# A two-layer encoder with expert-choice experts in fp32: nine row blocks in the second weight home, its first load in five pieces, a shorter router, later scaling of the norm weights, and the last head one expert later

## The reference

```python
def expert_choice_ffn(h, router_w, wg, wu, wd):
    C = max(1, EC_CAPACITY_FACTOR * S // N_EXPERTS)          # 2*256/16 = 32
    aff = jax.nn.softmax((h @ router_w).astype(jnp.float32), axis=-1)
    gate, idx = lax.top_k(jnp.swapaxes(aff, 1, 2), C)
    xs = take tokens idx of h                                # (16, 32, 1024)
    a = jnp.einsum('becd,edf->becf', xs, wg)                 # 1024 -> 1408
    u = jnp.einsum('becd,edf->becf', xs, wu)
    o = jnp.einsum('becf,efd->becd', jax.nn.silu(a) * u, wd) * gate
    return scatter-add of o to the tokens idx
...
for l in range(DEPTH):
    xn = rms_norm(x, norm1_w[l]); cols = xn @ w_in[l]
    attn = mla_branch(...)        # q and k are RMS-normed with q_norm_w, k_norm_w
    hy = hyena_branch(...)
    merged = gates[:, :, 0] * (attn @ w_attn_branch[l]) + gates[:, :, 1] * (hy @ w_hyena_branch[l])
    x = x + merged @ w_out[l]
    x = x + expert_choice_ffn(rms_norm(x, norm2_w[l]), router_w[l], ...)
```

## Time and profile before

| | |
|---|---|
| median of 3 runs | 2019.53 us (2016.12 to 2020.48) |
| the profiled execution | 2022.94 us, of it the span 2019.3 us |
| PE busy | 1560.6 us (77%) |
| DVE / ACT / POOL busy | 563.2 / 289.1 / 45.7 us |
| queue q1 (SP's transfers) | 638.40 MB, 75.0% of 16 DMA engines |
| mean TensorE clock granted | 0.891 of full |

### The profile page before, as it was taken

One profiled execution on the slowest core, in us unless ns is written; L12 is line 12 of the kernel. 1 busy time (PEld: TensorE's weight loads), 2 busy tenths in 40 slices (PEclk: granted clock), 3 DMA queues, 4 the chain that ended last, 5 costly groups with the idle time before them and its releaser, 6 DMA issues.

```text
span 2019.3 us, 22260 instructions
## 1 busy us (share of the span) xinstructions
PE 1560.6 (77%) x9564; PEld 869.8 (43%) x9564; DVE 563.2 (28%) x1079; ACT 289.1 (14%) x602; POOL 45.7 (2%) x24
## 2 busy tenths in 40 slices
PE   7999999776656665675799999997766666666667
PEld 5687688432222232232256876884222222222222
DVE  2654782211211111111136547612111112111111
ACT  2243210100000000000032332101100000000000
POOL 0300100000000000000002000000000000000000
PEclk9999999897887887798899999998878878878879
DMA  8532054689999999999965221535999999999997
GB/s 290 192 121 84 1 215 181 242 353 433 431 436 430 434 431 430 431 438 433 410 227 229 84 84 49 232 156 209 427 438 424 435 436 435 423 434 437 435 432 316
DMA packets 24378, 644.04 MB, mean 319 GB/s; under 512 B 2672, under 2 KB 3696, under 8 KB 5104
## 3 DMA queue, kind: packets, MB, share of 16 engines
q1 hardware_dynamic: 23248, 638.40, 75.0%
q10 hardware_dynamic: 1056, 4.53, 0.8%
HBM read 641.88 MB, written 1.05 MB: 318 GB/s over the span
## 4 chain that ended last, share of the span: by engine, by line
DMA 49%; PE 47%; DVE 2%; issue 1%; DVEq 1%; ACT 0%; SPq 0%; ACTq 0%
DMA region<-w_down_dram 47%; PE ps L831 11%; PE ps L462 7%; PE ps L529 6%; PE ps L669 5%; PE ps L742 3%; PE ps L490 2%; DMA qkw<-qkw_dram 2%; PE ps L652 1%; PE ps L605 1%; PE ps L552 1%; PE ps L507 1%; PE ps L641 1%; PE ps L790 1%; PE ps L576 1%; PE ps L544 1%
## 5 line engine op out<-in xcount | busy, mean ns | idle before, releaser
L790 PE MATMUL ps<-ring,uT 128*32 128x384 f32 (+1 forms) x3328 | 337.4, 541 | 261.5 <-DMA ring<-w_gbu_dram 254.1
L790 PEld LDWEIGHTS ps<-ring,uT 128*32 128x32 f32 x3328 | 139.9, 125 | 454.0 <-DMA ring<-w_gbu_dram 272.9
L831 PE MATMUL ps<-region,uT 128*32 128x512 f32 x1408 | 225.0, 760 | 94.7 <-DMA region<-w_down_dram 92.1
L1416 DVE TENSOR_TENSOR uT<-uT,ps 128x256 f32<-128x256 f32 x32 | 13.5, 421 | 625.8 <-PE ps L790 625.8
L462 PE MATMUL ps<-xnT,ring 128*128 128x256 f32 x768 | 178.3, 380 | 4.3 <-DVE uT L1074 2.6
L831 PEld LDWEIGHTS ps<-region,uT 128*32 128x32 f32 x1408 | 55.9, 135 | 241.5 <-issue 160.1
L462 PEld LDWEIGHTS ps<-xnT,ring 128*128 128x128 f32 x768 | 140.6, 190 | 23.9 <-DVE uT L1074 4.4
L846 PE MATMUL ps<-uT 128*128 128x512 f32 x256 | 124.1, 617 | 27.6 <-ACT uT L1058 21.6
L1052 ACT ACT_TABLE_LOAD x32 | 41.1, 1283 | 664.9 <-PE ps L790 664.9
L529 PE MATMUL ps<-xnT,ring 128*128 128x256 f32 x512 | 115.8, 380 | 0.0
L1422 DVE COPY uT<-ps 128x512 f32<-128x512 f32 x32 | 22.1, 691 | 303.6 <-PE ps L831 303.6
(11 more groups left out here) (198 smaller groups left out, 1459.8 us busy)
## 6 DMA issues: line engine op xcount, KB each, us to landing
ring<-w_gbu_dram SPq DMA_DIRECT2D x28, 7040.0 KB, 31.0
region<-w_down_dram SPq DMA_DIRECT2D x28, 5632.0 KB, 32.9
ring<-w_ga_dram SPq DMA_DIRECT2D x16, 4224.0 KB, 28.1
region<-w_ga_dram SPq DMA_DIRECT2D x16, 4224.0 KB, 33.4
ring<-units_dram SPq DMA_DIRECT2D x28, 2048.0 KB, 8.1
region<-w_down_dram SPq DMA_DIRECT2D x8, 2048.0 KB, 12.6
region<-units_dram SPq DMA_DIRECT2D x6, 2048.0 KB, 12.3
ring<-w_gbu_dram SPq DMA_DIRECT2D x2, 4992.0 KB, 14.8
```

Of the source, the lines that this page charges most:

```text
L790: m = mm(bank(b, QW[j], rows=CAP, row0=CAP * j), xs[:, i, q * CAP:(q + 1) * CAP], w[i][:, j * FT:j * FT + QW[j]], start=i == 0, stop=i == ...
L831: m = mm(bank(c, rows=CAP, row0=CAP * j), hT[:, b * P + CAP * j:b * P + CAP * (j + 1)], wd[:, CT * b + j, c * 512:(c + 1) * 512], start=b ...
```

## The change

1. **Head of nine row blocks.** `IA` becomes 9: the head now holds all 8 gate row blocks and the first of up (12672 columns), and `w_gbu` only the other 7 of up (9856 columns). The second home in `region` grows over the region's end into what was `uT`, which now lies right behind in the same tensor; the expert scratch (`xs`, `o_sb` and others) is moved 2944 columns on (`SCR`), and a few small tiles to a tensor `late`. `gate_a` is now signalled after the first up row block; a new `gate_h` after gate row block 4.
2. **First load of the second home (head 1) in five pieces**, as its parts come free: 3584 columns after the sixth merged block, 5120 after the eighth, 1024 and 896 behind the down weights of expert 0, and 2048 after the router's first product. **Head 2** comes in two pieces, after `gate_h` and `gate_a` of expert 0.
3. **Last head one expert later**: head 15 is started in the loop's turn 15 ahead of `w_gbu` 15, no longer in turn 14.
4. **Router**: the search reads PSUM directly (no copy); no running sum along tokens on DVE: the marked array is transposed first (PE), compared with 0 (DVE, 128x32), and summed by two matmuls with a triangular and an all-ones matrix. `lgT` is copied ahead of the reciprocal; ACT does its second pair of scaled copies ahead of the second pair of squares. PE runs 4 extra matmuls of 256 columns (`WARM`) whose result nobody reads, once the normalised x is there.
5. **xs in halves**: gate row blocks 0 to 3 wait only for the first half of `xs`.
6. **Norm weights**: the scaling of the q norm weights stands behind the first sine argument.

```diff
-IA = 6
-UP_TAIL = IA - (DB - IA)
+IA = DB + 1
+UP_TAIL = 5
...
-                load_gate_a(0)
+                load_gate_a_first(slice(UNIT, A_COLS))
                 unit_is_used(11)
                 unit_is_used(12)
                 sp.wait_ge(s["merged_dve"], L * 8 + 3)
-                load_gate_b_up_first(0)
+                load_gate_b_up(0)
+                sp.wait_ge(s["merged_dve"], L * 8 + 6)
+                load_gate_a_second(12 * 1024, 12 * 1024 + SPARE)
                 unit_is_used(13)
-                load_gate_b_up_first(1)
+                load_gate_a_first(slice(0, UNIT))
                 for b in range(FB):
                     unit_is_used(RING_UNITS + b)
                     load_down_block(0, b, wd_in[0])
+                    if b == 0:
+                        sp.wait_ge(s["merged_dve"], (L + 1) * 8)
+                        load_gate_a_second(REGION - 3072, REGION + 2048)
+                load_gate_a_second(NF_TILES * D, 12 * 1024)
+                load_gate_a_second(REGION + 2048, REGION + SCR)
                 sp.wait_ge(s["lgT_psum"], L + 1)
-                sp.wait_ge(s["norm2_rms"], L + 1)
-                load_gate_a(1)
+                load_gate_a_second(12 * 1024 + SPARE, REGION - 3072)
                 for e in range(1, E):
-                    if e < E - 1:
+                    if e == 1:
+                        sp.wait_ge(s["gate_h"], L * E + 1)
+                        load_gate_a_third(slice(0, 4 * FF), s["wga_third_in"])
+                        sp.wait_ge(s["gate_a"], L * E + 1)
+                        load_gate_a_third(slice(4 * FF, A_COLS), wga_in[0])
+                    elif e < E - 2:
                         sp.wait_ge(s["gate_a"], L * E + e)
                         load_gate_a(e + 1)
+                    elif e == E - 1:
+                        sp.wait_ge(s["gate_a"], L * E + e - 1)
+                        load_gate_a(e)
...
+                pe.wait_ge(s["xn2_act"], L + 1)
+                for _ in range(WARM):
+                    mm(bank(0, S), ident, xn2[:, 0, 0:S], start=True, stop=True)
+                pe.wait_ge(s["left_dve"], L + 1)
                 for t in range(SB):
-                    m = tp(bank(7, E, t * E), ptok[:, t * P:(t + 1) * P], ident[0:E, 0:E])
-                m.then_inc(s["pos_psum"], 1)
+                    m = tp(bank(7, E, t * E), work[:, t * P:(t + 1) * P], ident[0:E, 0:E])
+                m.then_inc(s["leftT_psum"], 1)
+                pe.wait_ge(s["picked_dve"], L + 1)
+                tri = cst[:, C_TRI:C_TRI + P]
+                mm(bank(6, SB * E, S), tri, picked, start=True, stop=False)
+                mm(bank(6, E, S + E), ones.to_broadcast([P, P]), picked[:, 0:E], start=False,
+                   stop=True).then_inc(s["rank_psum"], 1)
...
-                        for i in range(IA):
+                        for i in range(DB):
+                            if q == 0 and i % 4 == 0:
+                                pe.wait_ge(s["xs_dve"], 2 * (L * NG + g) + i // 4 + 1 + FREE)
                             m = product(2, wg[q % 2], i)
-                        m.then_inc(s["gate_a"], 1)
+                            if i == 3:
+                                m.then_inc(s["gate_h"], 1)
...
-                        for i in range(DB):
+                        product(3, wu[q % 2], 0).then_inc(s["gate_a"], 1)
+                        pe.wait_ge(s["wgbu_in"], 16 * (L * E + 1 + e))
+                        for i in range(1, DB):
...
-                dve.wait_ge(s["qkw_in"], 16 * (L + 1))
-                ts(qkw[:, 0:QK], qkw[:, 0:QK], QK ** -0.5, None, ALU.mult).then_inc(s["qkw_scaled"], 1)
...
                 sine_argument(L, 0)
+                dve.wait_ge(s["qkw_in"], 16 * (L + 1))
+                ts(qkw[:, 0:QK], qkw[:, 0:QK], QK ** -0.5, None, ALU.mult).then_inc(s["qkw_scaled"], 1)
```

More of the change, by code:

```diff
@@ L41 @@
 HW = 512
+WARM = 4
 EPS = 1e-6
@@ L84 @@
 C_FEAT = C_IF + 4 * P
-C_N = C_FEAT + S
+C_TRI = C_FEAT + S
+C_N = C_TRI + P
 NK = NF // 4
@@ L120, in build @@
         xnT_t = sb("xnT", DB * S)
-        uT_t = sb("uT", 24 * S)
+        uT_t = region[:, REGION:REGION + 24 * S]
+        late = sb("late", FT + 80)
         cst = sb("consts", C_N)
@@ L168, in build @@
         mT = uT_t[:, 2048:4096].rearrange("p (i s) -> p i s", s=S)
[L170 to L185 removed]
+        xs = uT_t[:, SCR:SCR + 1024].rearrange("p (i c) -> p i c", i=DB)
+        o_sb = uT_t[:, SCR + 1024:SCR + 2048]
+        gsel = uT_t[:, SCR + 2048:SCR + 2304].rearrange("p (b c) -> p b c", b=SB)
+        gselT = uT_t[:, SCR + 2304:SCR + 2560]
+        sil = uT_t[:, SCR + 2560:SCR + 2560 + FT]
+        hid_e = sil
+        pick = uT_t[:, SCR + 2560 + FT:SCR + 2816 + FT].rearrange("p (b c) -> p b c", b=SB)
+        hT = late[:, 0:FT]
+        lgT = o_sb[:, 0:S]
+        work = o_sb[0:E, S:2 * S]
+        picked = o_sb[:, 2 * S:2 * S + SB * E]
+        top8 = late[0:E, FT:FT + 8]
+        aff = late[:, FT + 16:FT + 16 + SB * E].rearrange("p (b e) -> p b e", b=SB)
+        pos = late[:, FT + 48:FT + 48 + SB * E].rearrange("p (b e) -> p b e", b=SB)
         ones = cst[:, C_ONES:C_ONES + 1]
@@ L205, in build @@
         ksq_rows = aT_t[:, :].rearrange("p (r c) -> p r c", c=NOPE)
-        pos_flat = uT_t[:, 5440:5440 + SB * E]
+        pos_flat = late[:, FT + 48:FT + 48 + SB * E]
         sg = [ring[:, M1AT + i * 512:M1AT + (i + 1) * 512] for i in range(3)]
@@ L1373, in _ @@
                 dve.wait_ge(s["affT_psum"], L + 1)
-                copy(work, bank(6, S, rows=E))
-                dve.drain()
-                for _ in range(CAP // 8):
-                    nc.vector.max(top8, work)
-                    dve.drain()
-                    nc.vector.match_replace(work, top8, work, -1.0)
-                    dve.drain()
-                ts(picked, work, 0.0, None, ALU.is_lt)
-                dve.drain()
-                nc.vector.tensor_tensor_scan(rank, picked, picked, 0.0, ALU.add, ALU.max)
-                dve.drain()
-                tt(ptok, rank, picked, ALU.mult).then_inc(s["pos_dve"], 1)
-                dve.wait_ge(s["pos_psum"], L + 1)
-                copy(pos_flat, bank(7, SB * E))
+                left = bank(6, S, rows=E)
+                for _ in range(CAP // 8):
+                    nc.vector.max(top8, left)
+                    dve.drain()
+                    m = nc.vector.match_replace(work, top8, left, -1.0)
+                    dve.drain()
+                    left = work
+                m.then_inc(s["left_dve"], 1)
+                dve.wait_ge(s["leftT_psum"], L + 1)
+                ts(picked, bank(7, SB * E), 0.0, None, ALU.is_lt).then_inc(s["picked_dve"], 1)
+                dve.wait_ge(s["rank_psum"], L + 1)
+                dve.drain()
+                tt(pos_flat, picked, bank(6, SB * E, S), ALU.mult)
                 dve.drain()
```

81 lines of the change are left out of this document (35 added, 46 removed).

## The result

| | before | after |
|---|---|---|
| median, us, run beside each other | 2020.01 (2016.12 to 2020.86) | 2004.08 (2002.85 to 2007.65, 4 runs) |
| profiled execution, us | 2022.94 | 2007.65 |
| its span, us | 2019.3 | 2005.8 |

The changed kernel takes 0.9927 of the time, 95% interval 0.9915 to 0.994. That is faster, as forecast, but 9 us above the 1995.0 and just outside the range, whose end was 2004.0. The traced execution, 2007.65 us, is the slowest of the four.

The account below looks back on a forecast made before the run. An unbroken stream of expert weight transfers was taken to bound the kernel. Layer 0's start 5.5, 8.35 per layer twice (16.7) and clock 2.5 made 24.7 us off the 2019.53 median: forecast 1995, range 1988 to 2004.

Parts of the forecast that it names:

- The larger head: Expert weight stream: head of nine row blocks loaded early leaves 4,224 fewer columns, 5.0 us per layer, ends 0 and 5.0.
- A hole in the DMA share: Expert stream: a DMA share below 0.95 around experts 1, 2 or 14 would show the forecast wrong.
- rival C: Expert stream: a late piece or half of head 2 stops it, losing 5.0 us per layer; 2004.8 us, chance 0.07.
- a step above 40.5 us: Expert stream: a step longer than 40.5 us, against 40.2 expected, would show the forecast wrong.
- the clock: Gathering after the router: extra matmuls lift PE to 2.4 GHz in one of two layers, 2.5 us, ends 0 and 5.0.
- the router: Router of each layer: no copy and ranking by two small matmuls let PE start gathering 1.1 us earlier.
- the start: Start of layer 0: no wait for norm weights and a higher clock bring the k/v product 5.5 us earlier.
- Last head one expert later: End of each layer's expert stream: the later head only moves slack; 0 us, ends 0 and -1 per layer.
- rival A: Gathering: PE's clock stays low in both layers, so 22.2 us are gained; 1997.3 us, chance 0.20.
- Head 2 and the halves of xs: Expert 0 in each layer: head 2 issued 1.3 us earlier at gate row block 4, half-xs wait saves 0.95 us.
- rival D: Expert stream: transfers run slower with the new row shapes; 3% slower gives 2031 us, chance 0.04.
- Rival B: Start of layer 0: another load is equally late, so the 5.5 us gain is lost; 2000.3 us, chance 0.07.

Follow-up runs that it names:

- e14: Changed kernel with 23 drains ahead of layer 0 and 2 in its last group, moving TensorE's loops 23 and 25 instructions further; 1997.61 us, one run.
- e9: Changed kernel with 56 drains ahead of layer 0 and 168 in its last group, moving TensorE's loops; 1996.08 us, 0.9887 of the kernel before.
- e15: Changed kernel with 48 drains ahead of layer 0, moving both TensorE loops 48 instructions further; 1997.35 us, one run.
- e11: Changed kernel without warming products, loops moved by 64 and 176 drains, last head issued in turn 14 again; 2001.0 us, 0.9912 of the kernel before.
- e10: Changed kernel itself, unmoved, once more in a program load of its own; 2005.81 us, 0.9932 of the kernel before.
- e8: Kernel before with only the norm weights' scaling moved behind the first sine argument on VectorE; 2013.86 us, 0.9971 of the kernel before.
- e13: Kernel before with 30 drains ahead of layer 0 and 10 in its last group, moving TensorE's loops; 2023.23 us, 1.0016 of the kernel before.
- e4: Kernel before with TensorE's three looped groups of experts written out, no jump back; 2023.15 us, 1.0023 of the kernel before.

## Why the prediction was wrong, point by point

**The larger head: the step that failed.** "4,224 fewer, x 1.19 ns = 5.0 us per layer" gave 10.0 us and brought 2.6 (1.72 + 0.92). As a price of columns the term was right only together with the late last head, 5.1 us at equal packets (see the next point). A hole in the DMA share, the sign I had named for rival C, did not appear: in windows of 40 us from 404 to 964 the share is 0.99 to 1.02. It dips to 0.89 and 0.90 at 930 to 940 in windows of 5 us, but e14, with the full gain, has such dips as well, 0.91 at 905 to 910 and at 930 to 935. My other sign, a step above 40.5 us, did appear. What failed is the sentence that this term rests on, "The expert part is a stream of transfers that does not stop", since a second user came into the stream. The changed kernel fetches 30 packets in each S, where the one before had 21 and 11. By the means of the table that is 4.3 us a layer over the level of 12; the kernel before had paid 1.2 of that once, in layer 0. e9, e14 and e15, where the same instructions stand elsewhere, show that it is the place of TensorE's loops. The change moved them by adding code ahead: the warming products, the ranking matmuls and their waits. I priced each such instruction by its duration alone. The trace of the kernel before could have warned me. Its 13 steps are not 40.23 us each, as I averaged them: eleven are 40.0 or 40.1, and the ones to the down products of experts 8 and 13 are 41.5 and 41.4. The first of these two stands right behind the wait of L779 on issue, so my own sign, a step above 40.5 us, was there already.

In the traces the change is 11.2 us short of the 24.7. Of that 7.4 are this term, 2.5 the clock and 1.5 the router; the start gave 0.4 more than forecast, and the rest is small.

**Last head one expert later: wrong.** I wrote that it only moves slack and took 0. By e11 it is worth 2.1 to 2.3 us of S in each layer; without it, the wider head would have brought 2.7 (598.3 to 595.6) and not 5.1. Two things that I treated apart, the wider head and the order at the end, pay only together.

**PE's clock: wrong, rival A.** I had counted one layer of two. The gathering took 6.20 and 6.52 us, and the row at 390 to 394 shows 0.50 under the last products and behind them. Over all runs of the new kernels the gathering of group 0 took 5.4 to 6.5 us with these products and 5.2 to 6.7 without. So 0 of the 2.5. The Trainium skill (TensorE: Matmul & The Clock Gate, Part 1) states that the point at which the clock rises varies from run to run of the same kernel; by it the 2.5 was a chance at most, and the changed kernel's own traces agree, with 6.20 and 6.52 us in the first and 6.29 and 5.99 in e10.

**Router: right direction, too large.** Forecast 1.1, measured 0.39 in layer 0 and 0.34 in layer 1. The ranking matmuls took 1.0 us instead of 0.6. The extra matmuls ended at 391.44, behind VectorE's last MATCH_REPLACE at 390.89, and stand on the chain. They cost there the 0 to 0.3 that I left out, and some 0.2 more. In e9, e14 and e15, with the same router, the gathering of layer 1 starts 0.8 to 0.9 us sooner than before, in e10 0.35; what makes the difference is open.

**Right.** The start of layer 0: 5.93 against 5.5, with the clock at 1.00 as forecast; e8, with this edit alone, is 6.3 us faster. That the number is so near is partly luck. The wait of 1.4 us for the consts did not come (L500 followed L494 without one), and L494 started at 37.24 instead of 36.2, since the block ahead of it came 1.2 us later than before. Head 2 and the halves of xs: head 2 was issued 2.73 us earlier than the start explains, against 3.35 forecast with the router's 1.1. PE begins expert 0 in layer 0 at once behind the gathering (394.45 + 6.20 = 400.65). The rate with the new shapes: 431 GB/s, steps of 40.07 us, so rival D is out. Rival B is out too. By the 358 GB/s of the Trainium skill (DMA: Bandwidth & Descriptors, Where 436 GB/s comes from) a step would take an estimated 48 us; the trace does not agree, with 40.07 us and 431 GB/s.

**The sum.** From before to e9 the traces give 24.4 us: 9.8 up to head 2, 6.1 and 4.8 in the two S, 3.8 between them. The forecast was 24.7. The start and the two front parts gave 13.6 where 5.5 + 6.7 + 2.5 = 14.7 were forecast, and the two S 10.9 instead of 10.0, since the kernel before had lost 1.2 to its own refetch in layer 0. The last landing of layer 0 was forecast at 993 us; it came at 992.9 in e9 and at 998.4 in the changed kernel. That e9 meets the forecast to 1.1 us is luck in part. The clock's 2.5 never came, and in its place stand the 1.2 and a start at which the second convolution block began at 28.96 instead of 30.34 us, with the same instructions as in the changed kernel.

## What to carry to other kernels

Where the DMA engines are full, look at the instruction queue's packet count and at waits "on issue" behind a loop's jump, before and after any edit, even one that only adds instructions ahead of the loop. If the count rises, move the loop by some tens of instructions and measure again before judging the edit. And price changes to a stream together with what happens at its end: bytes taken out of it are only worth something if the engine behind it is done by then.

## What the runs showed that I had not expected

- A loop of about 840 TensorE instructions (a matmul as two) stayed in the store or was fetched anew at each jump, depending on its place: ends of 2841, 2866, 2891 and 2899 stayed, 2843, 2851 and 2855 did not, 2825 and 2835 did both. 2841, 2866 and 2891 rest on one trace each. Why the bad band is so narrow, and what tips the cases at its edge, is open. Two more turns written out bring 12 more packets (24 against 12), so a turn is about six packets of program. If the store keeps whole packets, the place decides over how many of them a turn reaches; no run tests that.
- A miss stops TensorE for 5.8 + 3.4 us in the changed kernel and up to 7.5 + 4.4 in e13. Whether its packets wait behind the weight loads is not shown.
- A packet is 16 KB and takes about 1.05 us on its engine, which is 0.07 us of sixteen engines. In S 18 more of them cost 0.18 to 0.24 us each. Why so much more is not settled. The steps show it in lumps: a step of 41.2 to 41.6 us among steps of 40.0, one of them behind most missed jumps. Such a step alone is no proof of a miss: many stretches with 12 packets have one near their end, as at expert 13 in e14, 41.5 us.
- Fetching without any jump is not free either: e4, with its loops written out, is slower than the kernel before, 1.0023 (1.0013 to 1.0033).
